# Partition sums of the conditioning vectors: adding DMAs in a DRAM scratch in place of PE transposes and ScalarE sums, with the weight stream spread anew

## The chip, the cores and the metric

The kernel runs on one core of a Trainium2 chip. The metric is device time in microseconds (us), the median of the runs. All data is float32; most products are made of rounded high and low parts (float32r).

## What is computed

A token matrix x of 256 rows and 1024 columns goes through two blocks. The first has two mixer layers (three attention branches that read one projection, gates, an output projection). The second has four layers, each a mixer and a gated feed-forward part, and both parts of each layer are steered by six vectors of 1024 numbers that come from a conditioning vector c:

```python
c_act = jax.nn.silu(c)
for i in range(4):
    mod = c_act @ ada_w[i] + ada_b[i]            # 1024 x 6144 weights per layer
    sh1, sc1, g1, sh2, sc2, g2 = jnp.split(mod, 6, axis=-1)
    h = modulate(rmsnorm_2(x, norm_gain[i, 0]), sh1, sc1)   # h * (1 + scale) + shift
    y = mixer(h)                                  # swa, gla, fox, swa
    x = x + g1[:, None, :] * y
    h = modulate(rmsnorm_2(x, norm_gain[i, 1]), sh2, sc2)
    x = x + g2[:, None, :] * swiglu(h, ffn_w_gu[i], ffn_w_down[i])
```

The change concerns only how `mod` is made. It does not depend on x, so it can be made at any time before its layer.

## The kernel before

**One stream of weights.** All weights come from DRAM in pieces of 512 KB (two blocks of 128 rows by 512 columns) in one fixed order that `weight_stream` (L416) writes down. SyncE (SP) issues them into a ring of eight buffers (`raw`, `NRAW`); piece i waits until piece i-8 has been used. There are 640 pieces of the main products, called **tiles** here and numbered 0 to 639 in the order of use, and 192 pieces of `ada_w` (48 **groups** of 512 columns, four pieces each). `spread` puts the ada pieces between tiles, at an even rate over the places that it allows: the `dil` parts of the two mixer layers, and the feed-forward parts (`gu`, `dn`), but not the `diff`, `gate`, `swa`, `gla`, `fox` parts. A tile that is split in two column ranges is issued as two DMAs.

**What happens to a piece.** A tile is rounded by ScalarE (ACT) into `whi`; VectorE (DVE) makes the rest, `wlo = raw - whi`; then PE multiplies with it, in 24 products of 256 columns or 12 of 512. `refill` keeps at most five such tiles ready ahead of PE (`LOOK + 1`). An ada piece is used by DVE alone (`h_ada`): it multiplies the two blocks by a column of `c8` (silu(c) laid over the partitions) and adds them into an accumulator `pool` of 128 x 512. After the fourth piece of a group the accumulator holds, for 512 columns, 128 partial sums, one per partition, which remain to be added.

**How the partitions are summed.** `ada_sums` (L783) takes a finished group some tiles later: PE transposes the accumulator in four products of 128 x 128 against `ident_t` (`h_ada_tr`, L141 in the rows), ACT copies each into place with a sum along the row (`h_ada_sum`, ACTIVATE and ACTIVATION_READ_ACCUMULATOR), DVE adds the bias `adb` into `mod` (`h_ada_mod`). After the twelfth group of a layer DVE makes gain * (1 + scale) (`h_amod`), PE transposes `mod` once (`h_mod_T`), ACT copies it and GpSimd (POOL) writes it to the DRAM rows `mod_rows`. From there `mod_row` broadcasts each vector over the partitions when its layer needs it. A PSUM bank of the four `G` banks is held from the transposes until ACT has summed.

**Who sets the order.** Each engine's program is written by the same walk in Python. In the attention parts a small planner (`advance`, `filling`, `urgent`) keeps a clock per engine and places the steps of the attention units (`lg`, `tr`, `pv`: logits, transposes, values) between the tiles, when by its costs their inputs are ready; an ada piece counts 1.5 us on its DVE clock. At run time every engine runs its own order and waits on semaphores. `soon` holds steps that are to be written so many tiles later.

## Time and profile before

| | us |
|---|---|
| median of 3 runs | 2212.91 |
| lowest, highest | 2209.96, 2213.17 |
| span of the profiled execution (first to last instruction) | 2209.7 |
| PE busy | 2137.6 (97%) |
| DVE busy | 1567.3 (71%) |
| ACT busy | 1078.5 (49%) |
| POOL busy | 205.7 (9%) |
| moved by DMA | 472.47 MB, mean 214 GB/s |

The profiled execution's own time is not told apart from the runs; its span lies 0.3 us below the lowest and 3.2 us below the median, so that the time is the span and up to some 3 us around it. The profile's page has a line of tenths per engine over 40 equal slices, and the same for the DMA engines and their rate. A table of stretches gives for each the busy time of every engine, with the granted TensorE clock (1.00 is 2.4 GHz), the share of time in which the 16 DMA engines are busy, and their rate. Busy spans of neighbouring instructions overlap a little, so that an engine that never rests can show more than its time. Rows of order of time give start, length, engine and operation.

### The profile page before, as it was taken

The page shows a single profiled execution, that of the slowest core. Times are in us where ns is not written, and L with a number is a line of the kernel's source. Part 1 is how long each engine was busy: PE and PEld are TensorE (multiplying, and loading weights), DVE is VectorE, ACT ScalarE, POOL GpSimd, SP SyncE. Part 2 cuts the span into 40 slices and gives each one's busy share as a digit, 9 for nine tenths or more (in the row PEclk, how much of TensorE's full clock was granted, in tenths as well). Part 3 has the DMA queues.
Part 4 walks back from the last instruction along what each step waited for, and adds up shares of the span by engine and source line. Part 5 has one row for each costly group of instructions (what it writes and reads, how often), then busy time and mean ns, then how long its engine had stood idle before and what let it go on. Part 6 is the DMA issues. An engine that isn't in the chain of part 4 may idle for free. (4 is left out here: it accounts for less than half of the span.)

```text
span 2209.7 us, 34056 instructions
## 1 busy us (share of the span) xinstructions
PE 2137.6 (97%) x13639; PEld 1903.0 (86%) x13639; DVE 1567.3 (71%) x2159; ACT 1078.5 (49%) x2082; POOL 205.7 (9%) x244
## 2 busy tenths in 40 slices
PE   8999999999999999999999998999999999999997
PEld 7999888879988888777999887999897999788996
DVE  6578657766775676766998677899645895657454
ACT  5454555544455554454444543444455454454342
POOL 1101001101010011010001001001000001111010
PEclk9999999999999999999999999999999999999998
DMA  9878645567785455534899524899543897425551
GB/s 304 290 257 256 216 137 166 182 228 233 239 295 174 145 159 200 192 118 153 305 352 344 167 88 144 279 357 367 182 139 131 277 354 246 156 90 189 191 181 67
DMA packets 297284, 472.47 MB, mean 214 GB/s; under 512 B 20241, under 2 KB 153051, under 8 KB 297126
## 3 DMA queue, kind: packets, MB, share of 16 engines
q1 hardware_dynamic: 286566, 440.68, 59.2%
q0 software_dynamic: 10560, 29.61, 4.5%
q8 instruction: 108, 1.77, 0.3%
q14 instruction: 50, 0.41, 0.1%
HBM read 465.36 MB, written 4.85 MB: 213 GB/s over the span
## 5 line engine op out<-in xcount | busy, mean ns | idle before, releaser
L150 DVE TENSOR_TENSOR wlo<-raw,whi 128x1024 fp32r<-128x1024 f32 x640 | 774.3, 1237 | 204.0 <-ACT whi L144 201.9
L144 ACT ACTIVATE whi<-raw 128x1024 fp32r<-128x1024 f32 x640 | 648.9, 1057 | 161.4 <-DMA raw<-in_ffn_w_gu 68.7
L138 PE MATMUL G<-HTh,whi 128*128 128x256 f32 x2336 | 671.2, 287 | 9.7 <-ACT pool L144 7.0
L138 PE MATMUL G<-HTh,wlo 128*128 128x256 f32 x2336 | 661.6, 283 | 0.0
L138 PE MATMUL G<-HTl,whi 128*128 128x256 f32 x2336 | 661.5, 283 | 0.0
L138 PEld LDWEIGHTS G<-HTh,whi 128*128 128x128 f32 x2336 | 448.2, 192 | 18.3 <-issue 10.6
L138 PEld LDWEIGHTS G<-HTl,whi 128*128 128x128 f32 x2336 | 448.5, 192 | 2.1
L138 PEld LDWEIGHTS G<-HTh,wlo 128*128 128x128 f32 x2336 | 448.3, 192 | 0.0
L144 ACT ACTIVATE pool<-G 128x128 f32<-128x128 f32 (+2 forms) x400 | 165.9, 435 | 530.3 <-PE G L138 470.6
L138 PE MATMUL G<-whi,HTh 128*128 128x512 f32 (+1 forms) x784 | 314.5, 401 | 20.3 <-ACT HTh L144 10.7
L138 PE MATMUL G<-whi,HTl 128*128 128x512 f32 (+1 forms) x784 | 304.6, 388 | 4.2 <-DVE HTl L158 3.8
L138 PE MATMUL G<-wlo,HTh 128*128 128x512 f32 (+1 forms) x784 | 302.0, 385 | 0.0
L158 DVE SCALAR_TENSOR_TENSOR pool<-raw,c,pool 128x512 f32<-128x512 f32 x336 | 266.1, 792 | 7.6
L158 DVE SCALAR_TENSOR_TENSOR pool<-pool,G 128x512 f32<-128x512 f32 (+1 forms) x140 | 91.7, 656 | 164.4 <-ACT pool L144 133.3
L138 PEld LDWEIGHTS G<-whi,HTh 128*128 128x128 f32 x784 | 149.4, 191 | 56.4 <-DVE wlo L150 14.3
L138 PEld LDWEIGHTS G<-whi,HTl 128*128 128x128 f32 x784 | 149.0, 190 | 42.4 <-DVE HTl L158 12.9
L138 PEld LDWEIGHTS G<-wlo,HTh 128*128 128x128 f32 x784 | 149.5, 191 | 25.2
L138 PE MATMUL A<-whi,OTh 128*128 128x512 f32 x352 | 137.9, 392 | 1.1 <-DVE wlo L150 1.1
L138 PE MATMUL A<-wlo,OTh 128*128 128x512 f32 x352 | 137.5, 391 | 0.0
L138 PE MATMUL A<-whi,OTl 128*128 128x512 f32 x352 | 137.0, 389 | 0.0
L138 PE MATMUL G<-whi,OTh 128*128 128x512 f32 x272 | 109.0, 401 | 0.9 <-DVE HTl L158 0.9
L150 POOL TENSOR_TENSOR sm<-sm,mhalf 128x1 f32<-128x1 f32 (+1 forms) x44 | 50.0, 1138 | 618.0 <-DVE sm L155 606.9
(193 smaller groups left out, 2318.2 us busy)
## 6 DMA issues: line engine op xcount, KB each, us to landing
raw<-in_ada_w SPq DMA_DIRECT2D x192, 512.0 KB, 6.2
raw<-in_ffn_w_gu SPq DMA_DIRECT2D x352, 256.0 KB, 5.0
raw<-in_w_in SPq DMA_DIRECT2D x128, 512.0 KB, 4.6
raw<-in_ffn_w_down SPq DMA_DIRECT2D x88, 512.0 KB, 6.7
raw<-in_w_in SPq DMA_DIRECT2D x160, 256.0 KB, 4.5
raw<-in_swa_w_in SPq DMA_DIRECT2D x24, 512.0 KB, 5.1
pool<-mod_rows POOLq DMA_DIRECT2D x24, 512.0 KB, 6.4
raw<-in_gla_w_in SPq DMA_DIRECT2D x24, 512.0 KB, 4.9
```

The lines of the kernel that those rows point to most:

```text
L138: return self.e.matmul(out, a, b, start=start, stop=stop, skip_group_check=True) if self.e else self
L144: return self.e.activation(out, a, func, bias=bias, scale=scale, accum_out=accum) if self.e else self
L150: return self.e.tensor_tensor(out, a, b, op) if self.e else self
L158: return self.e.scalar_tensor_tensor(out=out, in0=a, scalar=s, in1=b, op0=op0, op1=op1) if self.e else self
```

## The change

An accumulator's 128 partitions are no longer added by PE and ACT, but in a DRAM scratch `mod_parts` of 64 rows per layer. SP writes partitions 0 to 63 of the accumulator there (128 KB); POOL then issues a DMA that adds partitions 64 to 127 to the same rows. After a layer's twelfth group four more adding DMAs, DRAM to DRAM, fold 64 rows to 32, 16, 8 and 4. POOL loads the four rows, the bias and the gains into an SBUF block of 48 partitions, DVE adds the five values per number in one reduction and makes gain * (1 + scale), and POOL writes the rows to `mod_rows`. The gains and biases are no longer transposed in the setup. The pool of blocks grows from 44 to 46; one condition on free banks in `gemm` is different for the last `gla` unit.

```diff
-    res = spread(layer1_pieces(I, 0) + layer1_pieces(I, 1), ada(0) + ada(1)[:18], 10, 24)
+    res = spread(layer1_pieces(I, 0) + layer1_pieces(I, 1), ada(0) + ada(1) + ada(2)[:10], 10, 24)
     for l in range(4):
-        extra = (ada(1)[18:] + ada(2)[:16], ada(2)[16:] + ada(3)[:16], ada(3)[16:], [])[l]
-        res += spread(layer2_pieces(I, l), extra, 0, (8, 8, 30, 0)[l])
+        extra = (ada(2)[10:44], ada(2)[44:] + ada(3)[:28], ada(3)[28:], [])[l]
+        res += spread(layer2_pieces(I, l), extra, 0, (8, 8, 50, 0)[l])
...
+        while self.adaq and self.adaq[0][4] <= i - NRAW:
+            self.ada_out(*self.adaq.pop(0)[:4])
...
+    def ada_out(self, l, u, b, acc):
+        n, rows = 12 * l + u, self.M.part[l][0:64, u * 512:u * 512 + 512]
+        wrote = (f"part{n % 3}", n)
+        before = [(f"part{n % 3}", n - 3)] if n > 2 else []
+        self.h_load("SP", wrote, rows, b.a[0:64, :], [acc] + before)
+
+        def add():
+            ev = (f"fold{n % 3}", n)
+            before = [(f"fold{n % 3}", n - 3)] if n > 2 else []
+            self.h_add(ev, rows, b.a[64:P, :], [wrote] + before)
+            b.release([ev])
+            self.sums.append(ev)
+            if u == 11:
+                self.soon += [[at, lambda h=h: self.fold(l, h)] for at, h in ((3, 32), (6, 16), (8, 8), (10, 4))]
+                self.soon += [[12, lambda: self.mod_load(l)]]
+        self.soon.append([2, add])
+
+    def fold(self, l, h):
+        part = self.M.part[l].rearrange("r (k c) -> (r k) c", c=2048)
+        ev = (f"half{l}", h)
+        self.h_add(ev, part[0:3 * h, :], part[3 * h:6 * h, :], self.sums)
+        self.sums = [ev]
...
-            if kk == 2:
-                self.ada_sums(4, 0)
...
-        for n in range(4):
-            mm = e.transpose(M.GB[g][:, n * P:n * P + P], b.a[:, n * P:n * P + P], M.ident[:, :])
...
-            op = e.activation(b.a[:, c], self.M.GB[g][:, c], ACT.Copy, accum=tot[:, n:n + 1])
```

In the stream, the first block's two mixer layers now hold 106 ada pieces (66 before), the feed-forward parts of the second block's layers 34, 32 and 20 (46, 48 and 32 before). Between tiles 28 and 63, the `dil` part of the first mixer layer, there are 45 (28 before), that is five for each four tiles; between tiles 156 and 191, the same part of the second layer, 44 (28 before). In the third layer's feed-forward part all 20 stand behind the seven tiles 498 to 504, as 2, 3, 3, 3, 3, 3, 3.

**SP in the first layer's `dil` part**, from tile 28 on. Before:

```order
L170 DMA raw<-in_ada_w 128x2x512
L170 DMA raw<-in_w_in 128x2x256 x4
L170 DMA raw<-in_ada_w 128x2x512
L170 DMA raw<-in_w_in 128x2x256 x2
L170 DMA raw<-in_ada_w 128x2x512
L170 DMA raw<-in_w_in 128x2x256 x2
```

Now:

```order
L173 DMA raw<-in_ada_w 128x2x512
L173 DMA raw<-in_w_in 128x2x256 x2
L173 DMA raw<-in_ada_w 128x2x512 x2
L173 DMA raw<-in_w_in 128x2x256 x2
L173 DMA mod_parts<-pool 64x512
L173 DMA raw<-in_ada_w 128x2x512
```

Two DMAs of `in_w_in` are one tile. Where a tile in four stood without an ada piece, one in four now has two, and the write of a finished group stands between them.

**DVE in the third layer's feed-forward part**, from tile 498 on (`wlo` is the rest of a tile, `pool<-raw,c` and `pool<-raw,c,pool` the two halves of an ada piece, `pool<-pool,G` the gated product). Before:

```order
L155 TENSOR_SCALAR pool<-raw,c 128x512
L158 SCALAR_TENSOR_TENSOR pool<-raw,c,pool 128x512
L150 TENSOR_TENSOR wlo<-raw,whi 128x1024
L158 SCALAR_TENSOR_TENSOR pool<-raw,c,pool 128x512 x2
L150 TENSOR_TENSOR wlo<-raw,whi 128x1024
L158 SCALAR_TENSOR_TENSOR pool<-pool,G 128x512 x2
L158 SCALAR_TENSOR_TENSOR pool<-raw,c,pool 128x512 x2
L150 TENSOR_TENSOR wlo<-raw,whi 128x1024
```

Now:

```order
L155 TENSOR_SCALAR pool<-raw,c 128x512
L158 SCALAR_TENSOR_TENSOR pool<-raw,c,pool 128x512 x3
L150 TENSOR_TENSOR wlo<-raw,whi 128x1024
L158 SCALAR_TENSOR_TENSOR pool<-raw,c,pool 128x512 x4
L155 TENSOR_SCALAR pool<-raw,c 128x512
L158 SCALAR_TENSOR_TENSOR pool<-raw,c,pool 128x512
L150 TENSOR_TENSOR wlo<-raw,whi 128x1024
L158 SCALAR_TENSOR_TENSOR pool<-pool,G 128x512 x2
L158 SCALAR_TENSOR_TENSOR pool<-raw,c,pool 128x512 x6
```

One ada piece stood before each tile's rest; now two or three do, for seven tiles, and none after that.

**POOL in the first block**, where the first layer's vectors are folded. Before:

```order
L150 TENSOR_TENSOR rmem<-sm,mhalf 128x1 x2
L170 DMA bias_scratch<-pool 20x16x512 x2
L150 TENSOR_TENSOR sm<-sm,mhalf 128x1 x2
L170 DMA bias_scratch<-pool 20x16x512 x2
L170 DMA kv_scratch<-pool 128x1024 x2
L170 DMA bias_t<-bias_scratch 64x384 x30
L150 TENSOR_TENSOR sm<-sm,mhalf 128x2
```

Now, from the third set of `bias_t` loads on:

```order
L173 DMA bias_t<-bias_scratch 64x384 x6
L170 DMA mod_parts<-pool 64x512 x2
L170 DMA mod_parts<-mod_parts 192x1024
L173 DMA bias_t<-bias_scratch 64x384 x6
L170 DMA mod_parts<-pool 64x512
L170 DMA mod_parts<-mod_parts 96x1024
L170 DMA mod_parts<-mod_parts 48x1024
L173 DMA bias_t<-bias_scratch 64x384 x6
L170 DMA mod_parts<-mod_parts 32x768
L173 DMA pool<-in_norm_gain 24x1x128 x2
```

The adding DMAs stand between the loads of the attention units' bias, and each fold waits on POOL's queue for the one before it to land.

On PE and the others the attention units of both mixer layers have moved as well. Before, the first two `dil` units of the first layer had all their steps between tiles 44 and 60; now only their first logits (tiles 55 and 56) stand ahead of tile 63, and the rest between tiles 63 and 69. From tile 90 on the units stand where they stood. In the second mixer layer it is alike, and its units stand up to eleven tiles later until tile 248. The order of the matrix products in the four layers of the second block is unchanged.

## Rows read from the trace of the kernel before

**Rows 1.** Page: busy time of each engine; rate of DMA by slice.

```profile
PE 2137.6 (97%) x13639; PEld 1903.0 (86%) x13639; DVE 1567.3 (71%) x2159; ACT 1078.5 (49%) x2082; POOL 205.7 (9%) x244
...
GB/s 304 290 257 256 216 137 166 182 228 233 239 295 174 145 159 200 192 118 153 305 352 344 167 88 144 279 357 367 182 139 131 277 354 246 156 90 189 191 181 67
```

**Rows 2.** Stretches: length, busy PE, PEld, DVE, ACT, POOL, clock, DMA share, GB/s.

```profile
103.77:234.80 131.03, 128.68 (x967) 123.61 (x966) 101.29 (x154) 67.90 (x152) 6.17 (x12) 1.00 0.82 266
234.80:328.42 93.62, 92.72 (x559) 81.31 (x558) 58.10 (x90) 50.32 (x95) 6.62 (x10) 1.00 0.48 152
534.90:667.20 132.30, 128.57 (x964) 123.25 (x963) 101.66 (x156) 66.60 (x145) 6.72 (x13) 1.00 0.81 264
...
1417.80:1553.40 135.60, 135.60 (x976) 128.39 (x975) 128.96 (x160) 69.82 (x162) 14.83 (x14) 1.00 1.02 359
1739.70:1830.00 90.30, 88.89 (x633) 83.64 (x632) 85.81 (x110) 44.40 (x105) 7.53 (x6) 1.00 1.00 347
...
2024.60:2166.30 141.70, 141.70 (x1011) 134.03 (x1010) 71.28 (x67) 58.83 (x67) 11.58 (x10) 1.00 0.57 187
```

**Rows 3.** PE in order of time, two groups' transposes in feed-forward: start, us.

```profile
1190.43 0.28 PE L138 MATMUL G<-HTh,wlo 128*128 128x256 f32 x1
1190.55 1.04 PE L141 MATMUL G<-ident_t,pool 128*128 128x128 f32 x8
1191.34 0.36 PE L138 MATMUL G<-HTh,whi 128*128 128x256 f32 x1
1191.54 0.28 PE L138 MATMUL G<-HTl,whi 128*128 128x256 f32 x1
```

**Rows 4.** PE in order of time, the last two groups.

```profile
1816.07 0.60 PE L141 MATMUL G<-ident_t,pool 128*128 128x128 f32 x4
1817.66 0.63 PE L141 MATMUL G<-ident_t,pool 128*128 128x128 f32 x4 [0.99 <-DVE pool L158]
1818.71 0.39 PE L138 MATMUL G<-HTh,whi 128*128 128x256 f32 x1 [0.42 <-DVE wlo L150]
```

**Rows 5.** PE in order of time, transpose of a layer's vectors.

```profile
618.69 0.27 PE L141 MATMUL G<-ident_t,mod 128*64 128x128 f32 x1
620.34 0.44 PE L141 MATMUL G<-ident_t,S 128*128 128x128 f32 x2 [1.38 <-ACT pool L144]
```

**Rows 6.** Chain that ended last: start, us; 24 or 12 products to a tile.

```profile
2098.56 5.47 PE A L138 x24
2104.02 11.51 PE G L138 x96
```

**Rows 7.** DVE in order of time, where it never rests.

```profile
1445.99 1.22 DVE L150 TENSOR_TENSOR wlo<-raw,whi 128x1024 fp32r<-128x1024 f32 x1
1447.13 0.48 DVE L155 TENSOR_SCALAR pool<-raw,c 128x512 f32<-128x512 f32 x1
1447.64 0.75 DVE L158 SCALAR_TENSOR_TENSOR pool<-raw,c,pool 128x512 f32<-128x512 f32 x1
1448.31 1.22 DVE L150 TENSOR_TENSOR wlo<-raw,whi 128x1024 fp32r<-128x1024 f32 x1
1449.45 1.53 DVE L158 SCALAR_TENSOR_TENSOR pool<-raw,c,pool 128x512 f32<-128x512 f32 x2
1450.90 1.22 DVE L150 TENSOR_TENSOR wlo<-raw,whi 128x1024 fp32r<-128x1024 f32 x1
```

**Rows 8.** DMA issues: count, KB each, median us from issue to landing.

```profile
raw<-in_ada_w SPq DMA_DIRECT2D x192, 512.0 KB, 6.2
...
kv_scratch<-pool POOLq DMA_DIRECT2D x2, 512.0 KB, 8.6
pool<-kv_scratch POOLq DMA_DIRECT2D x2, 512.0 KB, 4.2
```

**Rows 9.** PE in order of time, steps of two `dil` units.

```profile
198.29 1.46 PE L138 MATMUL A<-pool 128*128 128x256 f32 x6
199.58 0.60 PE L141 MATMUL A<-ident_t,S 128*128 128x128 f32 x4
199.94 0.36 PE L138 MATMUL G<-HTh,whi 128*128 128x256 f32 x1
...
208.74 2.75 PE L138 MATMUL A<-W,pool 128*128 128x256 f32 x12
```

**Rows 10.** Groups of instructions: count, busy us, mean ns.

```profile
L170 POOL DMA_DIRECT2D bias_t<-bias_scratch x80 | 41.9, 543 | 238.7 <-DVE S L158 238.2 <-issue 0.5
```

More of the change, by code:

```diff
@@ L167, in memset, with dma_add @@
         return self.e.memset(out, v) if self.e else self
+    def dma_add(self, out, a):
+        return self.e.dma_start(out, a, accum_op=ALU.add, max_dma_last_dim=4096) if self.e else self
     def dma_start(self, out, a):
@@ L717, in ada @@
         if k == 3:
-            self.adaq.append((l, u, self.acc, done, self.steps))
+            self.adaq.append((l, u, self.acc, done, p.i))
     def put(self, p):
@@ new lines, in fold, with mod_load, made @@
+    def fold(self, l, h):
[3 more added lines that the diff above has]
+        self.sums = [ev]
+    def mod_load(self, l):
+        M, b = self.M, self.mk_blk(4)
+        parts = b.a[0:48, 0:640].rearrange("a (r p) -> a r p", p=P)
+        gain = b.a[0:48, 768:896]
+        rows = M.part[l][0:4, :].rearrange("r (a p) -> a r p", p=P)
+        bias = M.I["ada_b_2"][l].rearrange("(a p) -> a p", p=P)
+        tg = [self.load("POOL", f"mg{l}{j}", b.a[24 * j:24 * j + 24, 768:896],
+                        M.I["norm_gain_2"][l][j].rearrange("(a p) -> a p", p=P).unsqueeze(0).to_broadcast([3, 8, P]), b.w)
+              for j in range(2)]
+        tb = self.load("POOL", f"mb{l}", parts[:, 4, :], bias, b.w)
+        tp = self.load("POOL", f"mp{l}", parts[:, 0:4, :], rows, b.w + self.sums)
+        self.sums = []
+        def made():
+            summed, scaled = ("ve_mod", (l, 0)), ("ve_mod", (l, 1))
+            self.h_mod(b.a[0:48, 640:768], parts.rearrange("a r p -> a p r"), gain, b.a[0:48, 896:1024], [tp, tb] + tg, summed, scaled)
+            self.mod_ev[l] = [self.load("POOL", f"mod{l}", M.mrows[l][0:48], b.a[0:48, 640:768], [summed])]
+            self.mod_ev[l] += [self.load("POOL", f"mod{l}{j}", M.mrows[l][48 + 8 * j:56 + 8 * j],
+                                         b.a[24 * j + 8:24 * j + 16, 896:1024], [scaled]) for j in range(2)]
+            b.release(self.mod_ev[l])
+        self.soon.append([3, made])
@@ L857, in gemm @@
                         self.evacuate(gs[g], evac, g, used)
-            if kk == 4 and self.modq and not all(self.gheld):
-                self.mod_rows()
             self.tick()
@@ L2694, in h_dil @@
             self.round_head(u, 4 + u["h"])
-    def h_ada_sum(self, g, b, summed, added, tot):
-        e = self.e
-        e.wait_ge(*self.at(summed))
-        for n in range(4):
-            c = slice(n * P, n * P + P)
-            op = e.activation(b.a[:, c], self.M.GB[g][:, c], ACT.Copy, accum=tot[:, n:n + 1])
-        op.then_inc(*self.up(added))
     def h_identr(self, tid, done):
@@ L2809, in h_ada, with h_mod @@
             op.then_inc(*self.up(done if c else ("ve_ada", (done[1], 0))))
-    def h_ada_mod(self, added, l, u, tot, done):
-        e, M = self.e, self.M
-        e.wait_ge(*self.at(self.tadb))
-        m, c = l * 64 + u * 4, l * 48 + u * 4
-        e.wait_ge(*self.at(added))
-        e.tensor_tensor(M.mod[:, m:m + 4], tot, M.adb[:, c:c + 4], ALU.add).then_inc(*self.up(done))
+    def h_mod(self, m, parts, gain, scaled, ready, summed, done):
+        e = self.e
+        for x in ready:
+            e.wait_ge(*self.at(x))
+        e.tensor_reduce(m, parts, ALU.add).then_inc(*self.up(summed))
+        e.wait_ge(*self.at(summed))
+        e.scalar_tensor_tensor(scaled, m, 1.0, gain, ALU.add, ALU.mult).then_inc(*self.up(done))
     def h_silu(self, out, ps, full, free, tanh, done):
@@ L3290, in h_load, with h_add @@
         self.e.dma_start(dst, src).then_inc(*self.up(ev, 16))
+    def h_add(self, ev, dst, src, waits):
+        for t in waits:
+            self.e.wait_ge(*self.at(t))
+        self.e.dma_add(dst, src).then_inc(*self.up(ev, 16))
     def h_pow(self, q, r, have, done):
```

112 lines of the change are left out of this document (21 added, 91 removed).

## The prediction

> **What bounds the kernel now.** I read the busy times first, then a table of stretches, then single rows. PE is busy 97% of the span, DVE 71%, ACT 49%, POOL 9% [rows 1]. The stretches tell more. In the feed-forward part of the second layer PE rests for nothing (135.60 of 135.60), although DVE is busy 128.96 and the DMA engines 1.02 at 359 GB/s; in the last layer, which has no ada pieces, PE is as full with DVE at half and the DMA engines at 0.57 [rows 2]. In the two `dil` parts PE idles 2.4 and 3.7 us of some 131, with DVE at 77% and DMA at 0.82 and 0.81 [rows 2]. So an instruction less on PE is time saved nearly everywhere, and the first question is what comes near PE where the stream gets denser. It is DMA and DVE that can: both were full in feed-forward at one ada piece a tile, and no slice of the page shows more than 367 GB/s [rows 1].
>
> **What is taken off PE.** Two groups' transposes between products of 256 columns: from 1190.55 to the second product after them at 1191.54 are 0.99 us, of which one product slot, 0.12 (1190.55 less 1190.43), is the product's own: 0.87 for two groups, 0.44 each [rows 3]. 48 groups give 20.9 us. The last two had to wait for their accumulator as well: 1816.07 to 1818.71, 2.64 in place of 0.87, so 1.8 more [rows 4]. The transpose of a layer's vectors held PE from 618.69 to 620.34, 1.65 us, of which 1.38 is a wait for ACT that may stay under another name [rows 5]; for the four I take 1. A few groups in the `dil` parts need 0.1 more; with that about **24.5 us off**. ACT loses 192 sums and DVE 48 small adds; both have idle time there, so nothing more is taken for it. The setup's smaller transposes are nothing beside it.
>
> **The denser `dil` parts.** First mixer layer, tiles 28 to 63, 131.03 us before. DMA moved 266 GB/s times 131.03, 34.9 MB [rows 2]. 17 more ada pieces of 0.524 MB are 8.9 MB. Eleven groups are written and added: a write of 0.131 MB, and an add that the trace does not show. Its lower bound is one more pass of 0.131 MB, its upper one three (source, destination, result): 2.9 to 5.8 MB in all. That is 46.7 to 49.6 MB; at 359 GB/s [rows 2] 130 to 138 us, at 367 [rows 1] 127 to 135. At tile 28 the stream is already five tiles and six ada pieces ahead (11 pieces, 16 us at that rate), and at the end it must only be as far ahead as a piece needs to land, 6.2 us [rows 8]: 10 us less, so 117 to 128.
>
> PE's own need there falls too: 131.0 less seven groups (3.1), less what moves behind tile 63. The second logits of two `dil` units are 1.29 each (198.29 to 199.58), twelve transposes 1.1 (four are 0.36), twelve value rows some 2.5 [rows 9]: 4.9 a unit, 9.8 for two. PE needs 118. DVE needs 101.29 plus 17 times 1.45 less the moved units, under 126 of busy spans that overlap by a tenth [rows 2, 7], about 115. So DMA asks 0 to 10 us more than PE; I take 4. Behind the part, PE was busy 92.72 of 93.62 [rows 2] and gets the 9.8 us back, which is no loss; but the units' steps now stand closer to each other (several of one unit within a tile), and their waits on ACT and DVE have fewer products between them. I take 2. The second mixer layer is alike with 16 more pieces. Together **12 us**, 0 to 24.
>
> One page bears on the add. The Trainium skill, "Collectives: The Full Stack", section "The bandwidth ceiling: the fold count and why AG ≠ RS ≠ AR", says that an add in the DMA path is slow not for its arithmetic but because it reads two sources. No run so far shows it; by it an add costs two passes, between my bounds, and the sum would be some 2 us lower than with three.
>
> **The third layer's feed-forward part.** `refill` lets DVE start on what precedes tile 499 when PE is at tile 494. Until tile 505 can start, DVE has 20 ada pieces, five of them a group's first at 1.18 (1447.13 to 1448.31) and fifteen at 1.45 (1449.45 to 1450.90), seven rests at 1.14, and two gated products, 1.2: 5.9, 21.8, 8.0 and 1.2, 36.9 us [rows 7]. PE needs for the eleven tiles seven times 2.88 and four times 2.73, 31.1 us [rows 6]. DVE is 5.8 us late, spread over the tiles 503 to 505. DMA has 27 pieces and three groups, some 43 us, but eight pieces of the ring are ahead, 12 us, so DVE ends last. Before, the same stretch had one piece a tile and lost only the 1.8 us counted above. **6 us**, 3 to 12; TensorE's clock was 1.00 throughout there [rows 2], and a fall of it beside a wait would cost little, since DVE would still be what PE waits for. The other two feed-forward parts get fewer pieces but had PE full already: nothing beyond the transposes.
>
> **Queues.** SP gets 48 more issues; each waits for an accumulator whose last piece the ring has already waited for, so nothing stands behind it. POOL gets 88 more DMAs at some 0.54 us of issue [rows 10], 48 us on an engine that is 91% idle. Each add waits for its write, and behind it on POOL stand bias loads, the small powers of the norms and the feed-forward rests. Each has tiles of time; I take 0, up to 8 (below). DVE may wait for a block that an add still reads: the block is given back by program about six tiles, 17 us, after the accumulator is done; 512 KB written and landed took 8.6 us [rows 8]; 0, at most 3.
>
> **Sum.** -24.5 + 12 + 6 is -6.5 us. The profiled span of 2209.7 becomes 2203; the time lies up to 3.2 us above the span, and against the median 2212.9 that is **2206 us**.
>
> **The rivals.**
>
> 1. *The denser parts are hidden.* The DMA engines could move more than the page's 367, since in feed-forward PE set their pace, not they; the unit steps that moved were placed by a planner that counts 1.5 us for each ada piece where rows show 1.18 to 1.45 [rows 7], so all inputs are early. For it speaks that PE lost nothing at share 1.00 and 1.02 [rows 2]. Then 24.5 are gained less 4 in the third feed-forward part: 2192.
>
> 2. *The adding DMAs take the engines' time: slower.* A write of 512 KB to DRAM landed in 8.6 us, the read of the same in 4.2 [rows 8]; if the passes of an add go at half the rate, each group costs 1.1 us more of all 16 engines than I count. In both `dil` parts 22 groups compete with a stream that has no slack left: 24 us, less what little PE has to spare there, 18. That gives 2224. It decides from 0.5 us a group on: 11 us more and the kernel is 4.4 us slower than before. Against it: the parts of a group are a quarter of an ada group's 2.1 MB even at my upper bound.
>
> 3. *The folds hold POOL.* A layer's first fold reads and writes 0.79 MB, 1.5 times what took 8.6 us to land [rows 8], so 13 us or more, and the next fold is written three tiles, 8.6 us, later and waits for it, with six loads of `bias_t` behind it. A unit then starts some 4 us late in each mixer layer and PE runs out of its steps' cover. In feed-forward the same waits have six tiles of room. 8 us: 2214, no change that can be told.
>
> **Chances.** The forecast 0.40 (its own range 2199 to 2212), rival 1 0.22, rival 2 0.28, rival 3 0.10. A measurement of this kernel tells 0.2%, 4.4 us, from no change. Rival 1 and three quarters of the forecast are faster by more: 0.52. Slower by more is nearly all of rival 2 beyond its threshold, 0.28; the rest of the forecast and rival 3 are within, 0.20. For eight in ten the range reaches from 2189, everything hidden, to 2225, rival 2 at its price.
>
> **What the changed profile would show.** No products on `ident_t` between the feed-forward products, and the second layer's feed-forward stretch shorter by some 5 us with PE still full (right about the transposes). The stretch of tiles 28 to 63 at 122 us with DMA share near 1 and PE idle 4 to 6 us (right about the overload); 118 with PE full is rival 1, 130 and more with PE waiting for `wlo` and ACT for `raw` is rival 2. Between tiles 498 and 505 three or four waits of PE for `wlo`, 6 us in all; none there makes that step wrong. Waits of POOL's folds on each other before `bias_t` loads, with DVE waiting for `bias_t`, are rival 3. The forecast is wrong at its root if adds land far later than a write of their size, or if PE's idle time grows where no ada piece was added.

## The result, and the profile after

The changed kernel takes **2299.6 us** (median of 4, 2298.2 to 2301.9) where the kernel before takes 2211.5 (2210.0 to 2213.2): 1.0404 times as long, 95% interval 1.0392 to 1.0417. The forecast was 2206, its range 2189 to 2225. The profiled execution has a span of 2298.3 us, 88.6 more than before.

The page after: busy times, then the granted clock and the DMA share by slices, and what HBM moved (to compare with [rows 1]).

```profile
span 2298.3 us, 33365 instructions
...
PE 2153.3 (94%) x13441; PEld 1909.8 (83%) x13441; DVE 1565.7 (68%) x2110; ACT 1025.5 (45%) x1694; POOL 272.3 (12%) x332
...
PEclk9999899999988999999999999999999999999999
DMA  9898855476887745553489843599644796535561
...
HBM read 471.72 MB, written 23.33 MB: 215 GB/s over the span
```

PE does less work and yet is busy longer (2153.3), and DVE and ACT have a smaller share than before. No engine got full. Stretches of after; columns as in [rows 2]. In this order they are tiles 28 to 63, 156 to 191, 192 to 219, most of the second layer's feed-forward part, and tiles 495 to 519:

```profile
104.46:273.14 168.68, 134.69 (x902) 126.85 (x901) 121.84 (x173) 60.27 (x91) 18.59 (x29) 0.89 0.84 268
580.59:757.79 177.20, 141.42 (x921) 133.56 (x919) 124.57 (x178) 60.12 (x95) 19.40 (x30) 0.87 0.82 263
757.79:860.28 102.49, 100.88 (x612) 88.93 (x611) 64.41 (x96) 48.80 (x85) 15.10 (x25) 1.00 0.58 180
1503.60:1640.00 136.40, 136.40 (x972) 128.90 (x971) 110.01 (x124) 57.58 (x66) 27.81 (x31) 1.00 1.02 345
1813.51:1897.88 84.37, 75.21 (x506) 69.55 (x505) 63.67 (x72) 28.35 (x32) 10.96 (x11) 0.96 0.94 303
```

The two `dil` parts are the loss: 131.03 became 168.68, and 132.30 became 177.20, together 82.5 us [rows 2]. PE idles 34.0 and 35.8 us there (2.35 and 3.73 before), which is 63.7 of it. Its busy time grew by 18.9, although transposes and steps of units left these stretches: the granted clock is 0.89 and 0.87 (1.00 before), so TensorE ran at its 1.2 GHz level for some 37 and 46 us (twice what is missing from 1.00, times the length). Neither DVE (72% and 70%) nor the DMA engines (0.84 and 0.82, 268 and 263 GB/s against the 359 of feed-forward) are full. So no engine is the limit over either part as a whole; something makes the engines wait for each other.

The clock's part can be seen over the whole program too: the same 13441 products keep PE busy 2153.3 us here and 2123.5 in e9 below, where only the order differs.

The same cut of other profiled executions, by tile (us between the first products of tiles; the experiments have their places below):

```
tiles            0-27   28-63  64-155  156-191  192-393  394-494  495-519  520-end
before          103.8   131.0   300.1    132.3    721.7    342.5     73.5    404.9
after           104.5   168.7   307.4    177.2    718.5    337.2     84.4    400.4
e9  cost 0.5    104.2   133.9   305.5    134.3    723.6    338.7     84.4    399.2
e13 e9, no adds 104.6   129.6   299.6    129.3    716.8    337.2     84.4    400.3
e12 before, 1.8 104.3   147.2   302.9    160.5    728.3    342.4     73.5    403.6
e17 best        104.7   134.7   300.3    133.5    715.8    337.4     73.6    400.1
```

What the waits are in both `dil` parts is told by the view of waits, here 112 to 300 us of after: engine, line, tile and the work it waited for, us in all, times, the longest.

```profile
ACT pool L144 <- PE G L138: 63.3, 12, 10.8
ACT whi L144 <- DMA raw<-in_w_in: 39.1, 17, 5.9
DVE wlo L150 <- ACT whi L144: 27.6, 16, 4.8
...
PE G L138 <- DVE wlo L150: 19.4, 7, 5.2
...
PE G L141 <- DVE S L155: 13.1, 3, 6.0
...
DVE pool L150 <- DMA mod_parts<-pool: 5.3, 2, 4.5
```

ACT waits for PE, DVE for ACT, and PE for DVE. PE has two such waits: for a tile's rest `wlo`, and for the `S` of an attention unit. Over both `dil` parts they are 35.8 us (19.4 and 16.4) and 29.5 us (13.1 and 16.4) of the 69.8 us that it idles. One turn of the wheel of the first kind, at tile 40, in order of time (start, us, in brackets the idle time before it and its releaser). First ACT, which copies a finished product out (`pool<-G`) and splits weights (`whi<-raw`):

```profile
142.78 1.06 ACT L144 ACTIVATE whi<-raw 128x1024 fp32r<-128x1024 f32 x1 [1.87 <-DMA raw<-in_w_in]
149.96 1.09 ACT L144 ACTIVATE pool<-G 128x512 f32<-128x512 f32 x2 [6.12 <-PE G L138]
150.93 2.00 ACT L144 ACTIVATE whi<-raw 128x1024 fp32r<-128x1024 f32 x2
```

then DVE and PE:

```profile
146.36 1.54 DVE L158 SCALAR_TENSOR_TENSOR pool<-raw,c,pool 128x512 f32<-128x512 f32 x2
152.02 1.23 DVE L150 TENSOR_TENSOR wlo<-raw,whi 128x1024 fp32r<-128x1024 f32 x1 [4.12 <-ACT whi L144]
```

```profile
153.30 0.39 PE L138 MATMUL G<-whi,HTh 128*128 128x256 f32 x1 [3.38 <-DVE wlo L150]
```

ACT stood idle for 6.12 us at the copy of PE's product, with two splits queued behind it that then waited for nothing. By the landings of the trace the raw weights of tile 40 had come at 145.44 and those of tile 41 at 148.59, and their splits began at 150.93 and 151.88. PE ended the product at 149.9, and from there everything ran in a chain: two copies, 1.09, one split, about 1.0, one rest on DVE, 1.23; that is PE's wait of 3.38. Not every tile is so: 16 of the 30 splits of tiles 34 to 63 began as soon as their raw weights landed. The ring is part of the wheel, since a buffer is filled again only after its rest. In the kernel before the same copies come at 148.78, ACT had waited 2.74, but the splits of the next tiles stood ahead of them:

```profile
148.78 1.09 ACT L144 ACTIVATE pool<-G 128x512 f32<-128x512 f32 x2 [2.74 <-PE G L138]
149.75 0.60 ACT L144 ACTIVATE W<-A 128x512 f32<-128x512 f32 x1
150.23 2.97 ACT L144 ACTIVATE whi<-raw 128x1024 fp32r<-128x1024 f32 x3
```

Here PE lost nothing. The order of instructions on every engine is fixed when the program is built, by a planner with a clock of its own: it counts 1.5 us of DVE for an ada piece, 1.6 us between two landings, and 4.5 us from a free raw buffer to the landing of its next piece. Where by that clock a piece has not landed, its split is put off, at the latest until PE takes the tile. The **lead** of a split is the number of tiles by which it stands ahead of PE's own in the program.

### The profile page after: what moved, and what is told of

The parts are those of the page before. It is cut to its first block and busy times, and to the rows that moved or that the text cites. A ratio compares the mean times of both kernels' runs of the same rounds, so it can differ in the third digit from the quotient of the medians.

```text
span 2298.3 us, 33365 instructions
## 1 busy us (share of the span) xinstructions
PE 2153.3 (94%) x13441; PEld 1909.8 (83%) x13441; DVE 1565.7 (68%) x2110; ACT 1025.5 (45%) x1694; POOL 272.3 (12%) x332
## 3 DMA queue, kind: packets, MB, share of 16 engines
HBM read 471.72 MB, written 23.33 MB: 215 GB/s over the span
## 5 line engine op out<-in xcount | busy, mean ns | idle before, releaser
L138 PE MATMUL G<-HTl,whi 128*128 128x256 f32 x2336 | 670.0, 287 | 0.0
L138 PE MATMUL G<-HTh,wlo 128*128 128x256 f32 x2336 | 669.5, 287 | 0.0
L138 PEld LDWEIGHTS G<-HTh,whi 128*128 128x128 f32 x2336 | 457.5, 196 | 39.0 <-DVE wlo L150 29.7
L138 PEld LDWEIGHTS G<-HTl,whi 128*128 128x128 f32 x2336 | 457.6, 196 | 2.2
L138 PEld LDWEIGHTS G<-HTh,wlo 128*128 128x128 f32 x2336 | 457.3, 196 | 0.0
L144 ACT ACTIVATE pool<-G 128x512 f32<-128x512 f32 (+1 forms) x204 | 114.3, 579 | 600.8 <-PE G L138 581.4
L158 DVE SCALAR_TENSOR_TENSOR pool<-raw,c,pool 128x512 f32<-128x512 f32 x336 | 255.3, 760 | 10.5
L138 PEld LDWEIGHTS G<-whi,HTl 128*128 128x128 f32 x784 | 150.6, 192 | 42.8 <-DVE HTl L158 13.5
L150 POOL TENSOR_TENSOR OTl<-pool,OTh 128x512 fp32r<-128x512 f32 x36 | 49.5, 1375 | 527.3 <-ACT OTh L144 527.3
```

The source lines that it names most:

```text
L138: return self.e.matmul(out, a, b, start=start, stop=stop, skip_group_check=True) if self.e else self
L144: return self.e.activation(out, a, func, bias=bias, scale=scale, accum_out=accum) if self.e else self
L150: return self.e.tensor_tensor(out, a, b, op) if self.e else self
L158: return self.e.scalar_tensor_tensor(out=out, in0=a, scalar=s, in1=b, op0=op0, op1=op1) if self.e else self
```

## The experiments

e1 to e13 and e15 are one execution each. The kernel before, run beside them, took 2215.9 us on the chip of e1 to e4 and 2209.8 to 2210.9 on the others, and 2208.6 to 2213.6 in 15 executions on one chip; a difference of 5 us between two such runs is therefore not told from scatter.

### Is it the stream's density or the adding DMAs? (e1 to e4)

The first theory was that the stream itself, denser than a piece a tile, is the loss; its rival was the DRAM traffic of the adds. e1 is the kernel before with a nearly as dense stream, e2 the changed kernel with the same, e3 a thinner one.

```diff
-    res = spread(layer1_pieces(I, 0) + layer1_pieces(I, 1), ada(0) + ada(1) + ada(2)[:10], 10, 24)
+    allp = ada(0, 1, 2, 3)
+    res = spread(layer1_pieces(I, 0) + layer1_pieces(I, 1), allp[:98], 10, 24)
...
-        extra = (ada(2)[10:44], ada(2)[44:] + ada(3)[:28], ada(3)[28:], [])[l]
-        res += spread(layer2_pieces(I, l), extra, 0, (8, 8, 30, 0)[l])
+        extra = (allp[98:140], allp[140:172], allp[172:], [])[l]
+        res += spread(layer2_pieces(I, l), extra, 0, (8, 8, 50, 0)[l])
```

> The kernel before (transposes on PE, ScalarE sums, no adding DMAs), with its ada pieces spread almost as densely as after: 98 of the 192 in the first block in place of 66 (106 after, for which this kernel has not enough pool blocks), the three feed-forward parts 42, 32 and 20. Theory 'density' (the stream itself, at more than one ada piece a tile, is what costs the time, through the ring of 8 and the clock falls behind each wait): the two dil parts grow as after's do, 60 to 90 us in all, so 2270 to 2300. Theory 'adding DMAs' (the writes, adds and folds cost it): without them the denser stream costs little, 2215 to 2230.

> The changed kernel with the same stream as the run before this one: 98, 42, 32, 20 in place of 106, 34, 32, 20. 'Density': 24 us less than the kernel before with this stream, since only the transposes are gone, so 2245 to 2280, and less than after's 2300. 'Adding DMAs': far above the kernel before with this stream, 2280 to 2295.

> The changed kernel with 86, 50, 32 and 24 pieces. 'Density': the part of 28 to 63 has about one ada piece a tile, as feed-forward has, where PE was kept full; the loss falls by more than half, 2215 to 2245. 'Adding DMAs': as many adds in all, a few less in the dil parts, so 2270 to 2285.

Measured: 2304.6 (e1), 2290.5 (e2) and 2276.1 (e3). Without one adding DMA the kernel before loses 89 us to the spread. e2 is 14 faster than e1; by the two theories' sizes that would be the transposes less what the adds cost, but the orders differ too. The expectations did not part the theories cleanly: e1 is 5 us above the range of "density", and e2 and e3 fall into the ranges of "adding DMAs". e3 did not lose less than half, as "density" had it: 20 pieces more than before cost 60 us, and what the transposes gave on top. 38 of these are in the two `dil` parts.

e4 leaves the writes, adds and folds out of the changed kernel.

```diff
-        self.h_load("SP", wrote, rows, b.a[0:64, :], [acc] + before)
...
-            self.h_add(ev, rows, b.a[64:P, :], [wrote] + before)
-            b.release([ev])
-            self.sums.append(ev)
+            b.release([acc])
```

> The changed kernel with its own dense stream, but nothing is written to the DRAM scratch, added or folded there (48 writes, 48 adding DMAs and 16 folds left out; each layer's vectors are read from the bias, so the partition sums are not computed). Accumulators come free once their last piece is done. 'Density': 2285 to 2300, nearly all of the loss stays. 'Adding DMAs': 2190 to 2205.

Measured: 2289.9, as "density" had it. The adds are 10 us of the 88 by the two times, 14 if each is taken against the kernel before on its own chip (74 and 88 above it). Tiles 28 to 63 of e4:

```profile
105.67:267.86 162.19, 132.72 (x902) 125.10 (x901) 121.13 (x173) 59.70 (x91) 3.09 (x6) 0.91 0.75 250
```

### Which resource? (e5 to e8)

e5 loads half of each ada piece, e6 does half of DVE's work on each; the order of all instructions stays.

```diff
+            if self.stream[i][0] == "ada":
+                dst, src = dst[:, :, 0:256], src[:, :, 0:256]
             self.e.dma_start(dst, src).then_inc(*self.up((f"raw{r}", (i, n)), 16))
```

> The changed kernel, of whose ada pieces only the left half of the columns is loaded (256 of 512 KB each; DVE still works on whole pieces, the right halves holding what an earlier piece left, so the vectors are not the reference's). The order of all instructions stays. Theory 'transfers' (the denser stream asks the DMA engines for more than they move, and a ring of 8 can't hide it): most of the loss goes, 2195 to 2225. Theory 'DVE's turn' (DVE comes to the ada pieces late or does them ahead of what PE needs, whatever their bytes): 2275 to 2300.

```diff
-        for c in range(2):
-            cc = c8[:, 2 * k + c:2 * k + c + 1]
+        cc = c8[:, 2 * k:2 * k + 1]
```

> The changed kernel with one DVE operation for an ada piece in place of two (1024 of the products summed over half the rows, so the vectors are not the reference's); all transfers stay whole, and so does the order. 'DVE's turn': most of the loss goes, 2195 to 2235. 'Transfers': 2275 to 2300.

Measured: 2290.9 and 2285.4. Neither theory holds for most of the loss: with a quarter of the stretch's bytes gone (45.2 MB to 34.1), or a quarter of DVE's time (121.84 to 91.30), little comes back: 9 and 14 of the 88 us in all, 12 and 8 of the 82.5 in the two `dil` parts. Tiles 28 to 63 of e5, where the DMA engines are now at 0.71, and of e6, where DVE is busy 56%:

```profile
104.68:266.98 162.30, 134.69 (x902) 126.47 (x901) 121.33 (x173) 59.35 (x91) 18.63 (x29) 0.89 0.71 210
```

```profile
102.48:266.11 163.63, 133.31 (x903) 125.12 (x901) 91.30 (x131) 59.88 (x91) 18.94 (x29) 0.90 0.86 274
```

At tile 40 of e5 the wheel turns as in after, with ACT waiting longer, since it had less to wait for before (the raw weights of tile 40 had landed at 141.59 and were split at 149.46); ACT, DVE and PE:

```profile
148.49 1.08 ACT L144 ACTIVATE pool<-G 128x512 f32<-128x512 f32 x2 [7.91 <-PE G L138]
149.46 2.95 ACT L144 ACTIVATE whi<-raw 128x1024 fp32r<-128x1024 f32 x3
...
150.55 1.23 DVE L150 TENSOR_TENSOR wlo<-raw,whi 128x1024 fp32r<-128x1024 f32 x1 [4.75 <-ACT whi L144]
...
151.83 0.39 PE L138 MATMUL G<-whi,HTh 128*128 128x256 f32 x1 [3.38 <-DVE wlo L150]
```

Again 3.38 to the hundredth. e7 has more raw buffers, e8 nearly the old spread.

```diff
-NRAW = 8
-NSPL = 7
+NRAW = 10
+NSPL = 6
```

> The changed kernel with a ring of 10 raw buffers in place of 8, paid for with 6 in place of 7 pairs of split buffers. Theory 'ring depth' (with five ada pieces to four tiles 8 buffers are 3.5 tiles of lead, so one late release stops the stream): half of the loss goes or more, 2205 to 2255. If bytes or DVE alone set the pace, or 6 pairs of split buffers cost as much as the ring gives, 2280 to 2310.

```diff
-    res = spread(layer1_pieces(I, 0) + layer1_pieces(I, 1), ada(0) + ada(1) + ada(2)[:10], 10, 24)
+    allp = ada(0, 1, 2, 3)
+    res = spread(layer1_pieces(I, 0) + layer1_pieces(I, 1), allp[:74], 10, 24)
...
-                self.soon += [[at, lambda h=h: self.fold(l, h)] for at, h in ((3, 32), (6, 16), (8, 8), (10, 4))]
+                self.soon += [[at, lambda h=h: self.fold(l, h)] for at, h in ((2, 32), (4, 16), (6, 8), (8, 4))]
```

> The changed kernel with nearly the kernel before's spread: 74, 46, 48 and 24 pieces (66, 46, 48, 32 before); so that each layer's vectors are there in time the group's add comes one tile sooner, the folds 2, 4, 6 and 8 tiles behind in place of 3, 6, 8 and 10. 'Density' (shown by the first four runs) with a knee between 74 and 86: 2195 to 2210, faster than before by the transposes. If the loss grows from the first piece above 66 on as it does up to 86 (4 us a piece): 2220 to 2230.

In e8 the add also stands one tile behind its write in place of two, and a layer's loads and their sum come sooner.

Measured: 2316.5 and 2305.6, both outside all ranges given. The deeper ring doesn't help (with six pairs of split buffers to pay for it, which was not tried apart): its two `dil` parts take 24.6 us less than those of after, but the program as a whole is slower. e8 has only eight pieces more than the kernel before in the first block and loses 94 us, but it says less than it seems to: 53.5 of them are in the `dil` parts, and DVE waits there for blocks that an adding DMA reads, 43 us in all against 21 in after. What did point at a decision instead of a quantity, the order, is that half the bytes or half of DVE's work of a piece left most of the loss in place, in e5 with the same wait of 3.38. The lead of the splits, worked out from the programs, and what the two `dil` parts took together:

```
                          mean lead of tiles         of 72 tiles   both dil     time
                      30-39  40-49  50-59  60-69     at lead 0     parts, us     us
before                  2.7    2.8    1.9    2.6          0         263.3      2211.5
after                   1.2    0.1    1.5    1.2         40         345.9      2299.6
e1  before, 98          1.3    0.0    1.0    2.1         37         335.8      2304.6
e2  after, 98           1.3    0.0    0.6    1.3         45         326.2      2290.5
e3  after, 86           2.3    1.1    0.0    1.2         32         301.4      2276.1
e7  ring of 10          1.7    0.2    0.5    1.6         35         321.3      2316.5
e8  after, 74           2.7    2.8    0.4    0.7         19         316.8      2305.6
e9  cost 0.5            2.7    2.3    1.9    2.1          0         268.3      2225.8
e10 planner's clock     2.7    2.8    1.9    2.6          0         299.5      2254.4
e12 before, cost 1.8    2.7    2.5    0.3    2.3         20         307.7      2264.5
e17 best                2.7    2.8    2.6    2.8          0         268.2      2204.1
```

Every kernel with tiles at lead 0 loses 38 us or more in the two parts, those without lose 36 at most and mostly under 7. The count doesn't rank them: e3 with 32 such tiles loses 38, e8 with 19 loses 53.5, and e10 with none loses 36.

### Is it the order? (e9 to e12)

The work, bytes and stream of the changed kernel stay; one number of the planner changes (e9), or three (e10, and e11 with 98, 38, 36 and 20 pieces). e12 does the reverse to the kernel before.

```diff
-        p.land = self.landed = max(self.landed + 1.6, self.freed[r] + 4.5)
+        p.land = self.landed = max(self.landed + 1.2, self.freed[r] + 2.5)
...
-        self.freed[p.r] = self.spend("DVE", 1.5, p.land)
+        self.freed[p.r] = self.spend("DVE", 0.7, p.land)
```

(That is e11's; e9 has 0.5 in the last line and the first as it was, e10 1.0 in the last, e12 1.8 and the first as it was.)

> The changed kernel, the same work, transfers, stream and adding DMAs; only the planner's cost of an ada piece on DVE is 0.5 in place of 1.5 us, which alters nothing but the order in which ACT and DVE get their instructions. By it the splits of tiles 40 to 49 stand 2.3 tiles ahead of PE's tile in the program (0.1 with 1.5, 2.8 in the kernel before). Theory 'order' (ACT waits at a finished product with the next tiles' splits queued behind it, because the planner believes DVE and the ring late): most of the loss goes, 2195 to 2230. If the stream's density costs by what it asks of the engines, 2280 to 2310.

> The changed kernel with its own dense stream; the planner's clock has an ada piece at 1.0, 1.2 between two landings in place of 1.6, and 2.5 from a free buffer to its next piece in place of 4.5. Splits stand 2.8 tiles ahead at tiles 40 to 49 and 1.9 at 50 to 59, as in the kernel before. 'Order': 2190 to 2225, and less than the run before this one, since the lead is larger. Density as such: 2280 to 2310.

> 98, 38, 36 and 20 pieces and a planner's clock with an ada piece at 0.7, landings 1.2 apart and 2.5 behind a free buffer: splits stand 2.6 to 2.8 tiles ahead throughout both dil parts. 'Order': 2185 to 2205, faster than the kernel before, the transposes' 24 us less what the transfers ask beyond PE. Density as such: 2265 to 2290, as with this spread and the old clock.

> The kernel before with its own spread of 66, 46, 48, 32 and all its transposes; the planner's cost of an ada piece is 1.8 in place of 1.5 us, nothing else. Splits of tiles 50 to 59 and 180 to 189 then stand 0.3 tiles ahead in place of 1.9 and 1.8, those of 170 to 179 1.0 in place of 2.7. 'Order': this alone makes the kernel before slower, 2235 to 2270, though not a byte or an instruction is added. Density as such: 2205 to 2220.

Measured: **2225.8, 2254.4, 2218.4 and 2264.5**. e9 wins back 74 of 88 us without a byte or an instruction less, and e12 costs the kernel before 55 us without one more. Both are inside their ranges, and far beyond the scatter: the order is the cause of most of the loss. e11 came 13 us above the top of its range. Tiles 28 to 63 and 156 to 191 of e9:

```profile
104.24:238.15 133.91, 125.76 (x939) 120.56 (x937) 119.98 (x178) 60.67 (x95) 20.08 (x33) 1.00 1.01 333
543.69:678.03 134.34, 127.37 (x939) 121.94 (x937) 119.92 (x178) 59.95 (x95) 15.53 (x24) 0.99 1.01 329
```

Which part of the order it is, these runs don't separate. e9's expectation says that only ACT and DVE get another order, but in the built programs PE does too: between tiles 28 and 63, and 156 and 191, the attention units have 80 and 81 products in the kernel before, 56 and 68 in after, 80 and 80 in e9 and e10, and 72 and 65 in e12. Splits ahead of PE and units between its tiles come and go together, and so do PE's two kinds of waits: in e9 they are 3.6 us for `wlo` and 5.6 for `S`, in both parts together.

In e9 the DMA engines are full, and the clock is back at 1.00 and 0.99 without anything done for it. In e12, at tile 52, ACT, DVE and PE show the wait that after had, in a kernel with the old stream and the old sums:

```profile
190.09 1.09 ACT L144 ACTIVATE pool<-G 128x512 f32<-128x512 f32 x2 [5.70 <-PE G L138]
191.06 3.05 ACT L144 ACTIVATE whi<-raw 128x1024 fp32r<-128x1024 f32 x3
...
192.15 2.36 DVE L150 TENSOR_TENSOR wlo<-raw,whi 128x1024 fp32r<-128x1024 f32 x2 [6.05 <-ACT whi L144]
...
193.43 0.58 PE L138 MATMUL G<-HTh,whi 128*128 128x256 f32 x1 [3.38 <-DVE wlo L150]
```

e10 missed its expectation by 30 us: all its splits had their lead, but its waits are others, as between 112 and 250 us:

```profile
ACT whi L144 <- DMA raw<-in_w_in: 69.0, 26, 6.2
...
PE G L138 <- DVE wlo L150: 10.7, 2, 8.0
DVE pool L150 <- DMA mod_parts<-pool: 7.5, 2, 6.3
```

The one long wait of PE there goes with DVE waiting 6.3 for a pool block that an adding DMA still reads; how much of the 30 us is that and how much the lead of DVE's rests (1.1 tiles, 1.7 in e9) was not taken apart. The second alone is no explanation, since the kernel before has 1.2 with its thinner stream. Splits with their full lead are thus needed, but not enough: here ACT waits 69.0 us for raw weights to land.

### What do the adding DMAs cost once the order is right? (e13, e15, e16)

e13 is e9 without writes, adds and folds. e15 is the kernel before with e11's spread and planner, e16 the kernel before with its own spread and e11's planner.

> The changed kernel with the planner's 0.5 for an ada piece (2225.75 in the run with the adds), and without the 48 writes, the 48 adding DMAs and the 16 folds (each layer's vectors read from the bias, so the partition sums are not computed). Theory 'adding DMAs cost what is left': once the order is right both dil parts run at a DMA share of 1.0, so the bytes of writes and adds (18.5 MB of writes by the page) come on top: 2208 to 2218, 8 to 17 less. Theory 'the stream alone fills the engines': 2220 to 2226.

> The kernel before (transposes on PE) with 98, 38, 36 and 20 pieces and the same planner's clock as the changed kernel had at 2218.37 with this spread; only the way of the partition sums differs between the two. If the adding DMAs bring the transposes' 24 us: 2235 to 2245. If they take back most of it in the dil parts: 2215 to 2228.

> The kernel before with its own spread, 66, 46, 48 and 32, and only the planner's clock changed as in the candidate of this group. PE idled 6 us in both dil parts before and nothing in feed-forward, so 'order' has little to give here: 2203 to 2212. Above 2215 the new clock would be worse for the old spread; and what the candidate gains beyond this run is the adding DMAs' own.

Measured: 2203.5 (e13, 4.5 below the lower of its ranges), 2223.8 (e15) and 2211.6 (e16, beside 2210.9 of the kernel before on that chip, ratio to the kernel before 1.000, 0.9991 to 1.001). So in this order the adding DMAs cost 22 us (e9 less e13), against 10 to 14 with the bad order; that the waits of the wheel hid the rest is my reading, not shown. At equal spread and planner the new sums gain only 5.5 us over the old (e15 less e11, one execution each, so hardly more than scatter) of the 24 that the transposes are worth. And the planner alone gives the kernel before nothing.

By the table of tiles, the 22 us are 4.3 and 5.0 in the two `dil` parts and 6.0 and 6.8 in the two stretches behind them. One 7 us piece of it can be seen whole. e9 at tile 195, POOL first:

```profile
671.59 0.83 POOL L170 DMA_DIRECT2D mod_parts<-pool  x1 [11.70 <-DMA mod_parts<-pool]
677.95 0.82 POOL L170 DMA_DIRECT2D mod_parts<-mod_parts  x1 [5.53 <-DMA mod_parts<-pool]
678.50 6.53 POOL L173 DMA_DIRECT2D bias_t<-bias_scratch  x12
```

and then DVE and PE:

```profile
687.10 0.42 DVE L158 SCALAR_TENSOR_TENSOR S<-A,bias_t 128x256 f32<-128x256 f32 x1 [4.79 <-DMA bias_t<-bias_scratch]
...
696.19 0.79 PE L138 MATMUL G<-whi,HTh 128*128 128x512 f32 x1 [7.17 <-DVE wlo L150]
```

A fold waits 5.53 us on POOL's queue for the last add, twelve bias loads stand behind it, DVE waits for the first of them, and its next rests, behind that on DVE, come 7 us late for PE. That is rival 3, at about the size given for it, in one place. It belongs to e9's order and not to the adds as such: tiles 192 to 219 take 109.9 us in e9, 100.1 in e13, and 100.2 in e11 and e18, which have all the adds.

### Can it win? (e14, e17, e18)

e14 takes a spread of 90, 42, 44 and 16 with the planner of e11.

> The changed kernel with 90, 42, 44 and 16 pieces (last one 44 pieces before the end of its part in place of 50) and a planner's clock with an ada piece at 0.7, landings 1.2 apart and 2.5 behind a free buffer. The dil parts keep a little below what the DMA engines move, the burst of the third feed-forward part falls away. 'Order' with density as a small term: 2190 to 2205, faster than the kernel before. If the adding DMAs cost what the transposes cost: 2205 to 2215.

Measured: 2221.2, ratio 1.0043 (1.003 to 1.0057): a little slower than the kernel before, and above both ranges. The burst in the third feed-forward part was gone (tiles 500 to 519 took 56.7 us, 67.9 in e9), but tiles 320 to 339 took 71.4 in place of 57.4, and one wait for a layer's sums cost 10 us. Waits of DVE in the whole of e14:

```profile
DVE pool L155 <- DMA mod_parts<-pool: 16.6, 4, 6.7
DVE pool L161 <- DMA pool<-mod_parts: 11.4, 1, 11.4
```

Both are waits at the head of DVE's queue for a DMA that the planner doesn't clock. e17 gives a block back four tiles later in the program and asks for the sums two tiles later, with 98, 38, 40 and 16 pieces; e18 is e11 with these two edits alone.

```diff
-            b.release([ev])
+            self.soon.append([4, lambda: b.release([ev])])
             self.sums.append(ev)
...
-        self.soon.append([3, made])
+        self.soon.append([5, made])
```

> The changed kernel with 98, 38, 40 and 16 pieces (46 before the end of its part), the planner's clock of 0.7, 1.2 and 2.5, an accumulator's block given back four tiles later in the program, and the sum of a layer's parts asked of DVE five tiles behind its load in place of three. The last two take DVE's waits for adding DMAs and for the load (23.4 us in nine waits in the run with 98, 38, 36 and 20; 11.4 in one wait in the candidate before). If these waits are what is left of the loss: 2195 to 2208, faster than the kernel before. If the DMA engines' time for writes and adds is: 2210 to 2220, since the bytes stay.

> The changed kernel with 98, 38, 36 and 20 pieces and the planner's clock of 0.7, 1.2 and 2.5, as in the run that took 2218.37, and only the later release of the accumulators' blocks and the later sum of a layer's parts added. If DVE's waits for adding DMAs (23.4 us in nine waits in that run) lie on the path that sets the end: 2206 to 2212, and the rest of the way to 2204.1 is the burst of the third feed-forward part, about 8 us in the stretch of tiles 500 to 519. If those waits are hidden behind the full DMA engines: 2215 to 2219.

Measured: e18 2211.6 (ratio 1.0008, 0.9999 to 1.0018), e17 **2204.1 (ratio 0.9973, 0.9963 to 0.9983)**. Of the 14 us between e11 and e17 the later release with the later sum gives 7 and the spread 7, which is the burst (tiles 495 to 519, 84.1 in e18 and 73.6 in e17) for the most part. e17 is the only complete kernel here that is faster than the kernel before, by 6 us. Its DVE never waits for `mod_parts`. Its `dil` parts:

```profile
104.73:239.38 134.65, 128.66 (x938) 123.53 (x937) 117.07 (x173) 60.78 (x95) 20.40 (x34) 0.97 1.00 321
539.69:673.23 133.54, 127.29 (x938) 122.10 (x937) 117.17 (x173) 60.06 (x95) 20.43 (x34) 0.99 1.00 324
```

## Why the prediction was wrong, step by step

**Transposes, -24.5: right.** Tiles 394 to 494 became 5.3 us shorter with PE full (136.40 of 136.40), as forecast; that layer lost twelve groups' transposes, 5.3 at 0.44 each. With the order right and no adds (e13) all parts outside tiles 495 to 519 are together 19 shorter; the rest of the 24.5 was not taken apart.

**The denser `dil` parts, +12, range 0 to 24: this step failed.** They cost 82.5 us. The bytes were right: the sum had 46.7 to 49.6 MB less 10 us of lead, 43 to 46 MB, and with the order right (e9) 44.6 MB moved between tiles 28 and 63. Their rate was not: 333 GB/s at a share of 1.01 in place of 359 to 367, so that the stretch took 133.9 us where the sum had 117 to 128 (PE is busy 125.8 of them in e9, since the units' steps stand there again that the sum had put behind tile 63). But that is small beside the loss: in e9 both parts together take 5 us more than before, and 77.6 of the 82.5 are the order's. What failed is the part of the term that said "their waits on ACT and DVE have fewer products between them. I take 2", and, in rival 1, that the planner had placed everything early since it counts 1.5 us for a piece. Rows of the kernel before can't show that for another order: there the clock of 1.5, 1.6 and 4.5 had placed all splits with a lead. The prediction treated the order as given and asked only whether each engine could do its sum of work in time. But the planner's 1.5, 1.6 and 4.5 decide which instruction stands ahead of which, and with the denser stream they put splits behind copies that wait for PE, and units' steps behind tile 63. From there on waits are a chain of latencies that no sum of busy times shows. The sign of it was before me: the unit steps of both mixer layers had moved by whole units, and I priced the steps and not the reason for their moving. The lead of the splits could be counted in the changed program: 0.1 tiles in place of 2.8 for tiles 40 to 49. None of the three rivals had it, and the sign given for rival 2 (130 us and more, PE waiting for `wlo` and ACT for `raw`) came true without rival 2 being the cause: without any adds e4 still takes 162.2.

The Trainium skill, "PSUM — Partial Sum Buffer", section "Engine vs sequencer instructions", says that the queues of ScalarE, VectorE and GpSimdE are strictly first in, first out. The traces agree: ACT stood idle 6.12 us at a copy while the splits behind it had their raw weights for up to 5.5 us.

**The clock: no term for it in the `dil` parts.** That "a fall of it beside a wait would cost little" was said of the third feed-forward part alone; for the `dil` parts the prediction put it at nothing and said nothing of it. Beside PE's waits of 34.0 and 35.8 us the granted clock was 0.89 and 0.87, and PE's busy time rose by 18.9 us, more if the transposes that left are counted, and at most half of the 83 us at 1.2 GHz. It was a consequence: with the order right the clock is 1.00 and 0.99.

**The third feed-forward part, +6, range 3 to 12: right in place, too small.** Tiles 495 to 519 took 84.4 in place of 73.5, 10.9 more, although six groups' transposes (2.6) had left them, so that the term measures 13.5; e1, which keeps the transposes, has 88.5 there, 15.0 more. e13 shows the same 84.4 without adds. DVE was late by more than the 5.8 worked out, the DMA engines, which the sum held to be behind DVE, were at 1.06 and 366 GB/s between 1830.00 and 1869.39, and the granted clock there was 0.91. How the size divides among the three is open.

**Queues, 0, at most 3 for DVE and 8 for POOL: the terms were mis-sized.** DVE waited for blocks 19.7 and 13.2 us in all in after. In e11 it waited 23.4; taking those waits away gave 7 us (e11 to e18). The claim that a block is given back long after its accumulator is done left out that the add waits for its write, and for the adds before it, on POOL. Rival 3 is seen in one place of e9.

**Rival 2, 1.1 us for each group in the `dil` parts: too large, and wrong as the cause.** e9 less e13 is 9.3 us in the two `dil` parts, 0.4 for each of the 22 groups and not all of it engine time; the other 13 of the 22.3 are elsewhere, 10 of them in tiles 192 to 219. In after itself the adds cost 10 to 14 us. Where the stream is thinner they are hidden: tiles 400 to 439 take 113.4 us with and without them. The Trainium skill's rule of two sources for an add ("Collectives: The Full Stack", as cited above) can't be seen in the counters: e13 reads 465.82 MB from HBM and after 471.72, 5.9 more, which is the folds' source once (four layers by 0.786, 0.393, 0.197 and 0.098 MB); a read of each destination, 12 MB more, doesn't show there. Whether the counter holds such a read no run tells, so the rule is neither shown nor refuted here.

## What to carry to other kernels

When a change alters the input of a planner, the new order is part of the change: count in the built program how far the producers (splits, loads) stand ahead of the instruction that waits for them, before and after, ahead of any sum of bytes and busy times. The count is a warning and not a measure: e10 had all of the lead and still lost 36 us in its two parts. A loss that stays when either engine's cost is halved points at the order; one constant of the planner, changed alone, tells. And a DMA that frees a buffer needs a place in the planner's clock, or its buffer must come back late enough.

## What was not expected of the hardware

- The adding DMAs themselves are quick. From the DMA issues of after (count, KB each, median us from issue to landing): an add of 128 KB lands as a write does, and the folds in much the same time.

```profile
mod_parts<-pool SPq DMA_DIRECT2D x48, 128.0 KB, 6.0
mod_parts<-pool POOLq DMA_DIRECT2D x48, 128.0 KB, 5.9
...
mod_parts<-mod_parts POOLq DMA_DIRECT2D x4, 768.0 KB, 7.7
```

- The issue of an add holds POOL for 877 ns, a plain load of `bias_t` for 640 (groups of instructions of after: count, busy us, mean ns, idle time before).

```profile
L173 POOL DMA_DIRECT2D bias_t<-bias_scratch x80 | 43.5, 640 | 26.9 <-DVE S L158 26.9
L170 POOL DMA_DIRECT2D mod_parts<-pool x48 | 41.8, 877 | 343.5 <-DMA mod_parts<-pool 343.0 <-issue 0.4
```

- With the order right the `dil` parts ran at a DMA share of 1.01 and only 333 GB/s, where feed-forward reached 359 at 1.02 [rows 2]. The small adds are not the reason, since e13, without them, has 327 GB/s at 0.98; what is was not looked into.
